# A three-block transformer kernel: differential queries and keys by features, rotary rows exchanged by transfers, and the latent layer's first residual behind its last projections

## The reference

```python
def apply_rope(x, cos, sin):
    x1, x2 = jnp.split(x, 2, axis=-1)
    return jnp.concatenate([x1 * c - x2 * s, x2 * c + x1 * s], axis=-1)

def diff_attention(h, w_qkv, ..., cos, sin):
    q, k, v = jnp.split(h @ w_qkv, 3, axis=-1)
    q = q.reshape(b, s, 8, 2, 64); k = k.reshape(b, s, 8, 2, 64); v = v.reshape(b, s, 8, 128)
    q = jnp.concatenate([apply_rope(q[..., :16], cos, sin), q[..., 16:]], axis=-1)
    ...
    a = p[:, :, 0] - lam * p[:, :, 1]
```

## Time and profile before

| what | before |
| --- | --- |
| median of 3 runs | 1745.36 us (1744.45 to 1746.98) |
| the profiled execution's own time | 1745.7 us |
| its span, granted clock | 1743.9 us, 0.998 |
| PE busy | 1728.2 us, 99% of the span |
| DVE, ACT, POOL busy | 1091.1, 785.4, 134.5 us |
| read from HBM | 148.61 MB |

### The profile page before, as it was taken

How to read it: one execution, slowest core, us unless ns; L and a number is a source line. 1 busy time by engine, 2 the same in 40 slices (tenths; PEclk the granted TensorE clock), 3 DMA queues, 4 the chain that set the end, 5 groups by cost and what they waited for, 6 DMA issues and landing times.

```text
span 1743.9 us, 22594 instructions
## 1 busy us (share of the span) xinstructions
PE 1728.2 (99%) x8782; PEld 1460.0 (84%) x8782; DVE 1091.1 (63%) x1719; ACT 785.4 (45%) x1398; POOL 134.5 (8%) x138
## 2 busy tenths in 40 slices
PE   9999999999999999999999999999999999999998
PEld 7888888888888888888888888889898888888887
DVE  5788644344346666685864764665888676376375
ACT  5553532222235555544532432456876454244244
POOL 2003200000005100002000000022101200000000
PEclk9999999999999999999999999999999999999999
DMA  5212333333333221122333333323111233333341
GB/s 169 73 51 85 93 97 97 97 97 97 97 97 97 78 69 61 61 73 85 96 97 97 97 93 101 97 76 103 39 49 37 81 92 98 98 98 97 98 127 61
DMA packets 128355, 152.78 MB, mean 88 GB/s; under 512 B 9286, under 2 KB 101992, under 8 KB 128248
## 3 DMA queue, kind: packets, MB, share of 16 engines
q1 hardware_dynamic: 128088, 151.26, 28.3%
q10 hardware_dynamic: 160, 0.07, 0.0%
HBM read 148.61 MB, written 2.10 MB: 86 GB/s over the span
## 4 chain that ended last, share of the span: by engine, by line
PE 94%; DVE 3%; ACT 1%; issue 1%; DMA 1%; POOL 0%; ACTq 0%; DVEq 0%; POOLq 0%
PE bk L1908 24%; PE bk L1909 23%; PE bk L1910 23%; PE bk L1937 5%; PE bk L1939 4%; PE bk L1938 4%; PE bk L1913 4%; PE bk L2035 2%; PE bk L2069 1%; PE bk L2068 1%; PE bk L1996 1%; PE bk L2023 1%; DVE WL L2100 1%; PE bk L2025 0%; PE bk L2024 0%
## 5 line engine op out<-in xcount | busy, mean ns | idle before, releaser
L1908 PE MATMUL bk<-R,WH 128*128 128x512 f32 x1844 | 724.0, 393 | 1.8 <-DVE R L2106 1.6
L1910 PE MATMUL bk<-R,WL 128*128 128x512 f32 x1844 | 718.4, 390 | 0.0
L1909 PE MATMUL bk<-R,WH 128*128 128x512 f32 x1844 | 718.1, 389 | 0.0
L2100 DVE TENSOR_TENSOR WL<-RAW,WH 128x1024 fp32r<-128x1024 f32 (+4 forms) x278 | 343.7, 1237 | 483.2 <-ACT WH L2302 482.2
L2302 ACT ACTIVATE WH<-RAW 128x1024 fp32r<-128x1024 f32 (+4 forms) x278 | 288.0, 1036 | 604.3 <-PE bk L1910 546.6
L1908 PEld LDWEIGHTS bk<-R,WH 128*128 128x128 f32 x1844 | 346.8, 188 | 73.4 <-issue 2.2
L1910 PEld LDWEIGHTS bk<-R,WL 128*128 128x128 f32 x1844 | 346.4, 188 | 72.8
L1909 PEld LDWEIGHTS bk<-R,WH 128*128 128x128 f32 x1844 | 346.8, 188 | 68.9
L1937 PE MATMUL bk<-WH,R 128*128 128x256 f32 (+4 forms) x432 | 146.0, 338 | 0.3 <-DVE KT L2106 0.3
L1939 PE MATMUL bk<-WL,R 128*128 128x256 f32 (+4 forms) x432 | 140.7, 326 | 0.0
L1938 PE MATMUL bk<-WH,R 128*128 128x256 f32 (+4 forms) x432 | 140.5, 325 | 0.0
(11 more groups left out here) (170 smaller groups left out, 1503.6 us busy)
## 6 DMA issues: line engine op xcount, KB each, us to landing
RAW<-in_ffn_w_up_dram SPq DMA_DIRECT2D x176, 256.0 KB, 3.0
RAW<-in_ffn_w_down_dram SPq DMA_DIRECT2D x44, 512.0 KB, 3.7
RAW<-in_w_gate_dram SPq DMA_DIRECT2D x44, 256.0 KB, 2.8
RAW<-in_w_up_dram SPq DMA_DIRECT2D x44, 256.0 KB, 3.1
RAW<-in_w_down_dram SPq DMA_DIRECT2D x22, 512.0 KB, 3.7
RAW<-in_da_w_qkv_dram SPq DMA_DIRECT2D x32, 256.0 KB, 2.9
RAW<-in_w_out_dram SPq DMA_DIRECT2D x8, 512.0 KB, 3.6
RAW<-in_da_w_qkv_dram SPq DMA_DIRECT2D x8, 512.0 KB, 3.6
```

Of the source, the lines that this page charges most:

```text
L1908: e.matmul(dst, lh, rh, start=start, stop=False)
L1909: e.matmul(dst, lh, rl, start=False, stop=False)
L1910: return e.matmul(dst, ll, rh, start=False, stop=stop)
L2100: e.tensor_tensor(low, sides(st.n, RAW[:, r, 0:m]), high.bitcast(F32), ALU.subtract).then_inc(on["wlo_dve"], 1)
```

## The change

**Differential queries and keys.** They are now made by `gemm_f`, features by tokens, with the same chunks and the same number of matmuls. TOK0 and TOK1 are taken as flat strips of 512 columns: TOK1 holds the tables `cos` and `sin` (128x512 each, from a new constant `rot` of 512 KB loaded during the first feed-forward part), which `rot_spread` multiplies once by the norm's factor; the other strips are two "plain" (ring of 2), two "swapped" (ring of 2) and four "out" (ring of 4). The swapped strips are zeroed once by POOL. For each of the 16 pieces of 128 features, `ev_rotated` does: copy the bank to a plain strip (`rot_copy`, ACT); multiply the bank by `cos` into an out strip (`scaled`, DVE), which frees the bank; exchange rows 0 to 7 with 8 to 15 and 64 to 71 with 72 to 79 from the plain into the swapped strip by four transfers on SP (`rot_swap`); multiply the swapped strip by `sin` and add it to the out strip, full width, on POOL (`rot_mix`); split into halves. The `eighth`, `tok_qk`, the differential `rope` and its 64 transposes go.

**Latent part.** The residual product of group 0 moves from between the projections of groups 2 and 3 to behind those of group 3; its weight chunks move with it. `mask_key`, `tok_lat` and `tok_q` get waits for all groups' strips, since TOK is shared.

```diff
-            if g == 2:
-                plan_rows(m_o, 0, 2)
-        for g in (1, 2):
+        for g in (0, 1, 2):
             plan_rows(m_o, g * 256, 2)
...
+        def rotation(N):
+            emit("rot_load", after=[])
+            landing(s_rot, free_at["pe"] + 20000.0)
+            for x in rot.swapped.fr:
+                st = yield step("rot_zero", dst=rot.at(x), after=counts(tok_free))
+                x.free = [st.pool]
+            while N() is None or N().rooted is None:
+                yield None
+            b = yield from bank()
+            st = yield step("over", bank=b.i, r=N().r, after=counts([b.free, N().rooted]))
+            st = yield step("rot_spread", bank=b.i, after=[st.pe, (s_rot, 16)])
+            put_bank(b, st.dve)
+            rot.spread = st.dve
...
+            def ev_rotated(m, bk, done):
+                while rot.spread is None or m < 2 and G.Q[m].h is None:
+                    yield None
+                y, z, o = (yield from taken_from(rot.plain)), (yield from taken_from(rot.swapped)), (yield from taken_from(rot.out))
+                st = yield step("rot_copy", dst=rot.at(y), bank=bk.i, after=counts([done, y.free]))
+                copied = st.act
+                st = yield step("scaled", dst=rot.at(o), bank=bk.i, bc=rot.cos, after=counts([copied, o.free, rot.spread]))
+                put_bank(bk, st.dve)
+                which = z.i - rot.first_swapped
+                rot.swaps[which] += 64
+                landed_in = (s_swap[which], rot.swaps[which])
+                emit("rot_swap", src=rot.at(y), dst=rot.at(z), which=which, after=counts([copied, z.free]))
+                ready_at[id(landed_in[0]), landed_in[1]] = at_time(copied) + 2500.0
+                rot.plain.put(y, landed_in)
+                st = yield step("rot_mix", z=rot.at(z), o=rot.at(o), after=[landed_in, st.dve, rot.spread])
+                rot.swapped.put(z, st.pool)
+                if m < 2:
+                    lo = yield from split_pair(G.Q[m], rot.at(o), [st.pool], 0.125)
...
-            if kind == "fg":
-                yield from gemm_f(N.X, 8, 4, ev_turned)
-            else:
-                spawn(turn_in())
-                yield from gemm_t(N.X, 8, 512, ev_qk)
+            yield from gemm_f(N.X, 8, 4, ev_turned if kind == "fg" else ev_rotated)
...
-            if g == 2:
-                yield from till(before)
-                yield from residual(before.O, 2)
             if g == 3:
...
-            for g in (1, 2):
+            for g in (0, 1, 2):
                 yield from till(Ms[g])
                 yield from residual(Ms[g].O, 2)
...
+                elif st.kind == "rot_swap":
+                    for done in st.after:
+                        w.wait_ge(*done)
+                    for r in (0, 64):
+                        e.dma_start(st.dst[r:r + 8, :], st.src[r + 8:r + 16, :]).then_inc(s_swap[st.which], 16)
+                        e.dma_start(st.dst[r + 8:r + 16, :], st.src[r:r + 8, :]).then_inc(s_swap[st.which], 16)
...
+                elif k == "rot_mix":
+                    for done in st.after:
+                        w.wait_ge(*done)
+                    e.tensor_tensor(st.z, st.z, rot.sin, ALU.mult).then_inc(on["rot_mix_pool"], 1)
+                    w.wait_ge(on["rot_mix_pool"], st.pool0 + 1)
+                    e.tensor_tensor(st.o, st.o, st.z, ALU.add).then_inc(on["rot_mix_pool"], 1)
```

More of the change, by code:

```diff
@@ new lines, in ev_rotated @@
+                rot.swapped.put(z, st.pool)
+                if m < 2:
+                    lo = yield from split_pair(G.Q[m], rot.at(o), [st.pool], 0.125)
+                else:
+                    while before and not before.valued:
+                        yield None
+                    i = G.kbase + 4 * (m - 2)
+                    lo = yield from halves(KT[:, i, :], KT[:, i + 1, :], rot.at(o), [st.pool], None, [kfree[i + x] for x in range(4)])
+                    kready[i] = [lo]
+                rot.out.put(o, lo)
@@ L1264, in turn_q @@
+                G.ups.append(lo)
                 G.split += 1
                 G.turned = G.split == 4
[L1267 to L1278 removed]
+            yield from gemm_f(N.X, 8, 4, ev_turned if kind == "fg" else ev_rotated)
```

139 lines of the change are left out of this document (63 added, 76 removed).

## The result

| | before | after |
|---|---|---|
| median | 1745.69 us (4 runs) | 1755.91 us (4 runs, 1753.89 to 1756.45) |
| span of the profiled execution | 1743.9 us | 1753.9 us |
| ratio after to before | | 1.0058, 95% interval 1.0045 to 1.0070 |

The change costs 10.2 us. I had forecast 1742.3, and the range ended at 1748.5.

The account below looks back on a forecast made before the run. PE was taken as the bound, busy 99% of the span. From 1745.7 us: -7.0 transposes, +0.4 broadcast, +1.5 exchange and POOL, +2.0 latent residual gives 1742.6; less 0.3 for the median, 1742.3 us, range 1736.5 to 1748.5.

Parts of the forecast that it names:

- steps 1 to 4: Differential stage: product form 0, transposes gone -7.0 us, added broadcast +0.4, copies, cosines and halves 0; -6.6 together.
- The term of the transposes: Differential queries and keys: 64 transposes leave PE's path, four groups at 1.76 us, -7.0 us.
- step 2: The transposes that go, -7.0 us, including 0.09 us per batch for the slower handover to the first matmul behind.
- the broadcast: Four added PE transposes that spread the norm's factor for `rot_spread`, forecast at +0.4 us.
- Step 5: Exchange and POOL's mixes in the differential stage: chain covered, POOL's effect on DVE the open cost; +1.5 us (0 to 9).
- I take 3: Assumed time in us for an exchange's transfer to land, set nearest the small loads' 2.6, slowest 4.0.
- the chain fits, with about 2 us over: Copy, transfer, mixes and halves of a group's first key piece finish before its first scores, about 2 us to spare.
- The lock: POOL instructions block DVE through a shared port pair; 0.4 us lost per POOL instruction taken, up to 1.1 possible.
- POOL's 32 instructions hold DVE: Rival: in differential groups 1 to 3, 1.1 us lost per POOL instruction fills DVE; 11 us, 1752 us, chance 0.10.
- transfers land late: Rival: landing takes 5 us instead of 3, keys miss scores by 2 us in three groups; 1746.8 us, chance 0.12.
- Step 6: Latent residual moved: longer run without filler, waits grow from 2.6 to 4.2 us, clock falls once; +2.0 us (-4.3 to +6).
- The marks set for being wrong: Prediction counts as wrong if the differential stage gains less than 3 us or the latent stage gains.

Follow-up runs that it names:

- e18: e8 (neither transfers nor mixes, rotary part left out of the result) with the latent residual back in its old place: 1741.46 us, ratio 0.9977.
- e8: The changed kernel with neither transfers nor mixes; copy, multiply and halves alone, rotary part left out of the result: 1742.35 us, ratio 0.9983.
- e3: The changed kernel with one line moved, so each exchange is written down right behind the copy, ahead of the multiply: 1748.59 us, ratio 1.0026.
- e9: e3 with the planner told the measured price of an exchange, 4.05 us to landing and 2.65 us of SP, instead of 2.5 us: 1753.78 us, ratio 1.0043.
- e13: e11 with POOL's 32 mixing instructions put back, writing only the exchanged strips, with no half waiting for them: 1757.86 us, ratio 1.0072.
- e11: e7 (transfers, no mixes) with the planner told the measured price of an exchange, 4.05 us to landing: 1745.17 us, ratio 0.9998.
- e4: The changed kernel without the 64 transfers; POOL's mixes stay and work on the zeroed strips: 1751.62 us, ratio 1.0038.
- e7: e3 without POOL's mixes; transfers stay, halves wait for their landing, planner told 2.5 us, rotary part left out: 1758.58 us, ratio 1.0075.
- e1: The kernel before with only the latent residual moved behind the last projections: 1746.48 us, ratio 1.0007.
- e16: e3 with the latent residual back in its old place: 1746.98 us, ratio 1.0019.
- e2: The changed kernel with the latent residual put back where it was before: 1753.77 us, ratio 1.0049.
- e15: e9 with the planner also told that a piece's mixes hold DVE for 1.0 us, same instructions: 1754.60 us, ratio 1.0057.
- e12: e3 with each exchange's four transfers issued two by SP and two by ACT, planner told 2.75 us to landing: 1758.57 us, ratio 1.0076.

## Why the prediction was wrong

The account, in medians: steps 1 to 4 alone took 3.8 off (e18). The residual gave back 0.9 (e8). Exchange and mixes, in the order of e3, gave back 6.2 more, and the order of the changed kernel another 7.3. This adds up to 10.6, counted from the median of before in e18's set, 1745.27.

The traces give the same account on PE. The mark after stands 12.5 us behind that of e18 (802.19 and 789.70 us). PE's waits ahead of it are 9.7 us in place of 0.8, and behind the long wait, from 742.48 to about 747.4 us, PE ran at 1.2 GHz (the window 742.40 to 747.50 was granted 0.50), which costs half of that, 2.5 us. That is 11.4 of the 12.5.

- **Steps 1 to 4, forecast -6.6, measured -3.8.** The mark of e18 stands at 789.70 us, 3.1 before that of the kernel before. The term of the transposes was right: by the starts of PE's rows between 566 us and the mark, 64 transposes took 6.9 us before and are gone. What the prediction put at nothing is the rest of the order. PE has 18 more long steps in e18, of 0.28 to 0.41 us where 0.23 is usual, the handover that step 2 had seen (0.09 each): 70 against 56 among the 512-wide products on weights and 5 against 1 among the value products of that width. That is some 1.6 us. Two new waits of PE on DVE, of 0.6 and 0.2 us, make 0.8, and the broadcast 0.5. Less than 1 us is left open. The direction was right, and the size was reckoned as if the other steps would not change their order.
- **Step 5 is the step that failed**, forecast +1.5, measured +13.6 (after against e8). Four of its assumptions broke. First, "I take 3" for the transfer: an exchange is four transfers of 16 KB, SP takes 0.67 us for each, and from the first issue to the mix it is 4.0 to 4.1 us where nothing else holds the mix, 2.7 of which block SP for the next piece. I had seen SP's hold and asked only whether the weights came late. Second, "the chain fits, with about 2 us over" followed keys to their own scores. The long wait came through a neighbour: a half of the keys at the head of ACT's queue, with probabilities of another head behind it. Third, the cover for the lock was an average over 50 us. Fourth, step 5 counted no clock: behind the long wait the granted clock fell, 2.5 us, and in e9 and e13 it fell twice.
- **The lock's size was right, its place was not.** From the rows after, against those of e11: 8 x (1273 - 688) + 8 x (1037 - 688) + 29 x (1351 - 1251) + 28 x (246 - 162) ns = 12.7 us in 32 POOL instructions, 0.40 each, just what I took. (DVE's smaller groups add less than 1 us.) I spread it over DVE's idle time. But 7.5 of the 12.7 us fall on the halves of queries and keys, at the head of each group, where PE, ACT and DVE wait on one another in turn. The weight split's mean, my mark for the lock, rose only to 1.35 us, so it was the wrong place to look. In e13, 8 x (1398 - 688) + 8 x (1324 - 688) + 29 x (1374 - 1251) ns = 14.3 us of hold, with no half waiting for a mix, went with 12.7 us more, of which up to 4.3 may be the strip's; e4 and e9 put the mixes at 9.3 and 8.6. The time does not follow the sum of the hold: in e3 those four groups lose 12 us, nearly as much as after. What counts is which of PE's waits a hold lengthens, and whether the clock falls behind it. The rival "POOL's 32 instructions hold DVE" named the mechanism and gave 1752. (Its 3.7 us per group, "what the latent stage paid in one bad stretch", is 4.3 by step 6's own reckoning.) It needed "some 0.7 us lost per instruction" to decide; 0.40 was enough. The Trainium skill (SBUF — State Buffer, section "Who interferes with whom") says that a DVE instruction with two SBUF inputs contends with a GpSimd instruction that reads SBUF, and that the later one waits for the whole of the other. The rows at 670.99 us agree, for an instruction of 0.16 us too.
- **The rival "transfers land late"** had the right landing from copy to mix (5 us: the copy of 715.48 ends at 716.08, the mix starts at 721.06) and the wrong price. Without the mixes they cost 2.8 rightly planned (e11) and 16.2 wrongly planned (e7).
- **Step 6, forecast +2.0, measured 0.9 to 2.1** (e1, e8 against e18, e3 against e16, after against e2). The size was right and the mechanism was not. The waits grew only from 3.2 to 3.8 us in sum, and the fall of the clock, forecast to come once as before, did not come: the window 1225 to 1360 us after was granted 1.00, and the stretch of 0.83 in the earlier trace rows has no like after or in e1. By these two changes in the traces the stage should have gained some 1.1 us. That the move costs 0.9 to 2.1 all the same makes the forecast right by luck, and where these 2 to 3 us go is not shown.
- **The marks set for being wrong** were that the differential stage gains less than 3 us or the latent stage gains. The first was met by far: it lost 9.4.

What stays open: why three of e3's nine runs and three of e16's twelve took some 6 us more than the others. Their lower mean clock, 0.997 to 0.998, says that it fell in them too, but only runs without a fall were traced. And why the order of e3, planned with a wrong price, leaves PE with shorter waits than those of e9 and e15: the order decides which DVE instruction a mix meets, and the planner knows nothing of that; e15's crude price for it did not help.

## What to carry to other kernels

Where the queues' order comes from a planner with prices, a new operation's price must be measured before its cost can be: with 2.5 us in place of 4.05 for a landing, the same instructions took 13.4 us longer in e7 than in e11. A true price of one operation is not enough either: with the mixes on POOL, whose hold on DVE the planner does not know, it made e9 5.2 us slower than e3. Ask of each new wait not who needs its result but who stands behind it in its queue. And judge the cover of an engine at the place where the new work falls, at the head of a group just behind the projections, not by its idle share of a stage: DVE had 71 us idle in the stage, and in e13 14.3 us of hold still cost some 8.4 us or more. And price a wait of PE with the clock behind it: in e9 two waits of 1.7 and 1.6 us brought 3.6 us of lost clock.

## What the hardware showed that I had not expected

- A transfer of 16 KB from SBUF to SBUF takes SP 0.62 to 0.65 us to issue, more than the 0.37 us of a 512 KB weight load in the same queue (724.97 us), and POOL, which waits for the last of four, starts 1.4 us after its issue ended (716.98 + 2.65 to 721.06 us). The Trainium skill (DMA: Bandwidth & Descriptors, section "Rules for kernel authors") says that below 64 KB one pays mostly overhead; here two thirds of the 4.05 us, the 2.65 of issuing, were the issuing engine's.
- With two queues issuing at once (e12), the mix started 1.6 to 1.8 us behind the last issue in seven of the 16 pieces and 2.2 at the place shown, instead of 1.4, so that halving the issues brought 0.9 us, and at that place 0.4.
- DVE is held by POOL for the whole of POOL's instruction even when its own work is four columns: 0.16 us became 1.15 (670.99 us, above).
- The granted clock fell from 2.4 to 1.2 GHz behind short waits of PE: in e9 behind one of 1.70 and one of 1.58 us (0.91 over 20 us each), in the kernel before behind 0.79 and 1.03 us. Behind two waits of 1.4 us in e11 it did not fall, so the length of one wait does not decide it.
